# Hybrid encoder step on one core: six low parts per layer through an adding DMA, level products on one engine, other orders at a group's first down units

## What is computed

```python
hn = rmsnorm(x, n1)
proj = hn @ w_in                     # retention q,k,v,g | GLA q,k,v,g,gate | attention q,k,v
a = retention(...)                   # 4 heads, chunks of 64
b = gated_linear_attention(...)      # 4 heads, chunks of 64, decay from a cumulative log gate
c = band_attention(...)              # 8 heads, own chunk and the 8 before
x = x + concat(a, b, c) @ w_out
x = x + square(relu(rmsnorm(x, n2) @ w_up)) @ w_down     # width 4096 inside
```

## Time and profile before

| | us |
|---|---|
| median of 3 runs | 1393.74 (1393.55 to 1395.85) |
| the profiled execution, its own time | 1395.68 |
| its span, first to last instruction | 1393.9 |
| TensorE busy / VectorE / ScalarE / GpSimd | 1344.4 / 947.0 / 643.3 / 155.4 |
| mean granted TensorE clock | 0.991 of full speed |

### The profile page before, as it was taken

The page is one execution under the profiler, slowest core; times in us unless marked ns, Lnnn a source line. Parts: engine busy times, 40 slices in busy tenths (PEclk is TensorE's granted clock), DMA queues, the critical chain, the costliest instruction groups (busy, mean ns, idle before and its releaser), DMA issues. The chain is left out here.

```text
span 1393.9 us, 28762 instructions
## 1 busy us (share of the span) xinstructions
PE 1344.4 (96%) x12206; PEld 1300.3 (93%) x12206; DVE 947.0 (68%) x1480; ACT 643.3 (46%) x1051; POOL 155.4 (11%) x107
## 2 busy tenths in 40 slices
PE   8999999999999999999999999999999999999996
PEld 8899989899999999999998999888999999999995
DVE  6797766778667376575758967667874765746734
ACT  5423555656426236254424236566572362542731
POOL 0200000012120110200202000000201103012012
PEclk9999999999999999999999999999999999999998
DMA  6213333222322323223221223331222232222211
GB/s 227 71 64 103 97 101 116 77 91 76 107 92 78 105 77 106 91 78 105 79 76 48 68 85 120 126 103 63 91 89 95 76 107 91 84 99 92 99 54 64
DMA packets 50640, 127.83 MB, mean 92 GB/s; under 512 B 8401, under 2 KB 17745, under 8 KB 50513
## 3 DMA queue, kind: packets, MB, share of 16 engines
q1 hardware_dynamic: 50224, 125.44, 27.5%
q10 hardware_dynamic: 288, 0.55, 0.1%
HBM read 118.77 MB, written 7.21 MB: 90 GB/s over the span
## 5 line engine op out<-in xcount | busy, mean ns | idle before, releaser
L1698 PE MATMUL PS<-zhi,whi 128*128 128x272 f32 x1280 | 370.0, 289 | 14.0 <-DVE sq L1563 13.6
L1698 PE MATMUL PS<-zhi,wlo 128*128 128x272 f32 x1280 | 370.8, 290 | 0.0
L1698 PE MATMUL PS<-zlo,whi 128*128 128x272 f32 x1280 | 368.8, 288 | 0.0
L999 DVE TENSOR_TENSOR wlo<-raw,whi 128x1024 fp32r<-128x1024 f32 x136 | 169.1, 1243 | 178.3 <-ACT whi L554 177.4
L554 ACT ACTIVATE whi<-raw 128x1024 fp32r<-128x1024 f32 x136 | 143.3, 1055 | 300.1 <-PE PS L1698 295.1
L1698 PE MATMUL PS<-xhi,whi 128*128 128x272 f32 x896 | 271.0, 302 | 6.2 <-DVE wlo L999 3.2
L1698 PE MATMUL PS<-xhi,wlo 128*128 128x272 f32 x896 | 261.1, 291 | 0.0
L1698 PE MATMUL PS<-xlo,whi 128*128 128x272 f32 x896 | 260.5, 291 | 0.0
L1698 PEld LDWEIGHTS PS<-zhi,whi 128*128 128x128 f32 x1280 | 241.3, 188 | 16.1 <-DVE wlo L999 16.0
L1698 PEld LDWEIGHTS PS<-zlo,whi 128*128 128x128 f32 x1280 | 241.6, 189 | 0.0
L1698 PEld LDWEIGHTS PS<-zhi,wlo 128*128 128x128 f32 x1280 | 241.0, 188 | 0.0
(11 more groups left out here) (288 smaller groups left out, 2442.3 us busy)
## 6 DMA issues: line engine op xcount, KB each, us to landing
raw<-in_wu SPq DMA_DIRECT2D x199, 512.0 KB, 3.5
Bh<-in_bias SPq DMA_DIRECT2D x16, 256.0 KB, 4.1
h<-in_x SPq DMA_DIRECT2D x8, 272.0 KB, 6.3
out_k_t<-att_k SPq DMA_DIRECT2D x8, 272.0 KB, 4.3
out_y_t<-y SPq DMA_DIRECT2D x8, 272.0 KB, 2.7
kct<-in_ck SPq DMA_DIRECT2D x8, 256.0 KB, 3.3
cvb<-in_cv SPq DMA_DIRECT2D x8, 256.0 KB, 4.1
out_v_p<-vtk SPq DMA_DIRECT2D x8, 256.0 KB, 2.2
```

The lines of the kernel that those rows point to most:

```text
L999: nc.vector.tensor_tensor(wlo[n % SPL][:, :], raw[n % RAW][:, :], f32(whi[n % SPL][:, :]), ALU.subtract).then_inc(sems["w_lo"], 1)
L1698: return nc.tensor.matmul(out, lhsT, rhs, start=start, stop=stop, skip_group_check=True)
```

## The change

Three things are changed.

1. *Low parts by DMA.* For units 6 to 11 of each layer (`LO_DMA`) VectorE's `rest` is left out. ScalarE, right after `whi`, writes `-whi` into `wlo`; GpSimd then issues a DMA that reads the unit again from HBM and adds it onto `wlo`. `begin` waits for that DMA (semaphores `lo_in0`, `lo_in1`), and SP may load into `raw` again as soon as `whi` is there. Twelve DMAs of 512 KB are added in all.
2. *Levels.* `gk` and `gq` lie in one tile `gkq`, and one VectorE instruction per level makes both halves of `QK` (`level_qk`); GpSimd's `level` goes.
3. *Orders at a group's first down units.* TensorE now does only inputs 0 and 1 of `down+1` before the last two of `down`, and the other six after it. VectorE does `scaled(m - 1)` before `rest(down + m + 1)`. In the first group of a layer `r2` is made before the last pair's `add_c22`, not after the last `zlo`.

```diff
+LO_DMA = range(6, 12)
...
+def by_dma(unit):
+    return unit % UNITS in LO_DMA
...
                         old = unit - RAW
-                        if plain(old) is not None:
-                            sp.wait_ge(sems["w_lo"], plain(old) + 1)
+                        if by_dma(old):
+                            sp.wait_ge(sems["w_hi"], plain(old) + 1)
+                        elif plain(old) is not None:
+                            sp.wait_ge(sems["w_lo"], low(old)[1])
...
-                    def level(l):
...
-                            ins = nc.gpsimd.tensor_tensor(q[:, :, 0, :], f[:, :, 0, :], k[:, :, 0, :], ALU.mult)
-                        ins.then_inc(sems["qk_pool"], 1)
...
+                    for i, n in enumerate(LO_DMA):
+                        pool.wait_ge(sems["w_neg"], nth("w_neg", i + 1))
+                        nc.gpsimd.dma_start(wlo[n % SPL][:, :], wu[layer * UNITS + n, :, :], accum_op=ALU.add) \
+                            .then_inc(sems[f"lo_in{n % SPL}"], 16)
...
                         nc.scalar.activation(whi[n % SPL][:, :], raw[n % RAW][:, :], ACT.Copy).then_inc(sems["w_hi"], 1)
+                        if by_dma(unit):
+                            act.wait_ge(sems["w_hi"], i + 1)
+                            nc.scalar.activation(wlo[n % SPL][:, :], f32(whi[n % SPL][:, :]), ACT.Copy, scale=-1.0) \
+                                .then_inc(sems["w_neg"], 1)
...
-                            f, q, k = (blocks(t, c0, c1, H) for t in (F[l % 2], QK[l % 2], gq))
-                            ins = nc.vector.tensor_tensor(q[:, :, 1, :], f[:, :, 1, :], k[:, :, 1, :], ALU.mult)
-                        ins.then_inc(sems["qk_dve"], 1)
+                            f, qk = (blocks(t, c0, c1, H) for t in (F[l % 2], QK[l % 2]))
+                            kq = gkq[:, c0:c1]
+                            kq = bass.AP(kq.tensor, kq.offset, [kq.ap[0], (2 * H, (c1 - c0) // (2 * H)), (PW + H, 2), (1, H)])
+                            ins = nc.vector.tensor_tensor(qk, f, kq, ALU.mult)
+                        ins.then_inc(sems["qk_ready"], 1)
...
+                            if g == 0 and not more:
+                                dve.wait_ge(sems["ss_all"], nth("ss_all", 1))
+                                nc.vector.tensor_scalar(r2[:, :], rstd[:, :], 1.0 / D, EPS, ALU.mult, ALU.add) \
+                                    .then_inc(sems["r2_steps"], 1)
...
                             add_c22(j)
...
                         for m in range(1, KC):
+                            scaled(m - 1, g)
                             if m < KC - 1:
                                 rest(down + m + 1)
                             elif g == GROUPS - 1:
                                 rest(UNITS)
-                            scaled(m - 1, g)
...
                     def begin(n):
 
+                        name, count = low(layer * UNITS + n)
+                        pe.wait_ge(sems[name], count)
                         unit = plain(layer * UNITS + n)
-                        pe.wait_ge(sems["w_lo"], unit + 1)
...
                         pe.wait_ge(sems["c21"], layer * PAIRS + j)
-                        products(down + 1, (zhi, zlo), all_kc[:6], last=False)
+                        products(down + 1, (zhi, zlo), (0, 1), last=False)
                         products(down, (zhi, zlo), (6, 7), first=False, ready=z_ready)
-                        products(down + 1, (zhi, zlo), (6, 7), first=False)
+                        products(down + 1, (zhi, zlo), all_kc[2:], first=False)
```

More of the change, by code:

```diff
@@ L140, in plain, with low @@
     return None if k < KC else layer * PLAIN + UP + g * KC + k - KC
+def by_dma(unit):
+    return unit % UNITS in LO_DMA
+def low(unit):
+    layer, n = divmod(unit, UNITS)
+    before = min(max(n - LO_DMA.start, 0), len(LO_DMA))
+    if by_dma(unit):
+        return f"lo_in{n % SPL}", PER["lo_in0"] * layer + 16 * (before // SPL + 1)
+    return "w_lo", plain(unit) - len(LO_DMA) * layer - before + 1
 def pair_of(unit):
@@ L255, in hybrid_encoder @@
         Z = 4 * PW
-        gk, gq, gv, gb = (at(n, [P, PW], zone + i * Z) for i, n in enumerate(["gk", "gq", "gv", "gb"]))
+        gkq = at("gkq", [P, 2 * PW], zone)
+        gk, gq = gkq[:, 0:PW], gkq[:, PW:2 * PW]
+        gv, gb = (at(n, [P, PW], zone + i * Z) for i, n in ((2, "gv"), (3, "gb")))
         F = [at(f"F{i}", [P, PW], zone + (4 + i) * Z) for i in range(2)]
@@ L997, in rest @@
                             return
+                        if by_dma(unit):
+                            return
                         dve.wait_ge(sems["w_hi"], plain(unit) + 1)
@@ L1115, in level_x @@
                         if l >= 2:
[L1116 removed]
+                            dve.wait_ge(sems["qk_ready"], nth("qk_ready", l - 1))
                         for g, c0, c1 in level_parts(H):
@@ L1123, in level_x, with level_qk @@
                         ins.then_inc(sems["lev_x"], 1)
-                    def level_q(l):
+                    def level_qk(l):
                         H = LEVELS[l]
@@ L1175, in stage @@
                             if kind == GLA:
-                                level_q(0)
+                                level_qk(0)
                             dve.wait_ge(sems["pe_diag"], nth("pe_diag", kind + 1))
@@ L1200, in stage @@
                             if l + 1 < len(LEVELS):
-                                level_q(l + 1)
+                                level_qk(l + 1)
                             if l + 2 < len(LEVELS):
@@ L1601, in _ @@
                                 sum_s2(j + 1)
+                            if g == 0 and not more:
+                                dve.wait_ge(sems["ss_all"], nth("ss_all", 1))
+                                nc.vector.tensor_scalar(r2[:, :], rstd[:, :], 1.0 / D, EPS, ALU.mult, ALU.add) \
+                                    .then_inc(sems["r2_steps"], 1)
+                                for a in range(2):
+                                    c = slice(a * HT, (a + 1) * HT)
+                                    dve.wait_ge(sems["r2_steps"], nth("r2_steps", a + 1))
+                                    nc.vector.reciprocal(r2[:, c], r2[:, c]).then_inc(sems["r2_steps"], 1)
+                                dve.wait_ge(sems["r2_steps"], nth("r2_steps", 3))
                             add_c22(j)
```

23 lines of the change are left out of this document (6 added, 17 removed).

## The result

The changed kernel took 1373.05 us (median of four executions, 1372.16 to 1375.14) against 1393.64 for the kernel before on the same chip: a ratio of 0.985, 95% interval 0.983 to 0.987. Its profiled execution, the longest of the four, took 1375.14, with a span of 1373.3, 20.6 less than before (1393.9). The prediction was 1375.0 in a range of 1370 to 1388.

What follows compares the result with a forecast made beforehand. TensorE was taken as the bound (busy 1344.4 of 1393.9 us), so only its waits could give time: 1393.9 - 13.6 - 2.9 - 1.6 - 4.0 + 3.0 = 1374.8 of span, from the median 1374.6, say 1375; range 1370 to 1388.

Steps and rivals of the forecast that it cites:

- First down units, -13.6: First down units of the eight groups: TensorE's eight waits of 1.7 us for sq go, -13.6 us.
- Both margins of 0.5 us: In the groups: zlo rows 6 and 7, and c22 before product 4, each ready 0.5 us early, costed at nothing.
- Between the layers, -2.9 and -1.6: Layer boundary: the wait for xlo goes, -2.9 us, and the lower clock right behind it, 694 to 698, -1.6.
- The rival "more": Layer 1's GLA stage: the lower clock there goes too and nothing stalls, 1366 to 1370 us; chance 0.06.
- GLA, VectorE side, -4.0: GLA stage: fewer rest and merged level products shorten waits for QK, Ps and rk, -4.0 us (bounds 0 and -7).
- VectorE's instructions of two inputs there take 1.3 or less: GLA stage: a sign to look for, that VectorE's two-input instructions all take 1.3 us or less.
- The DMAs, +3.0: GLA stage: adding DMAs take 6.5 us, unit 6 stalls 1.4 and unit 10 0.1 a layer, +3.0 (0 to +9.4).
- The other four have over a microsecond more: GLA stage: the DMAs of units other than 6 and 10 have over a microsecond more cover.
- the 8 us: GLA stage, adding DMA: a latency from issue to landing over 8 us would show the prediction wrong.
- The bound of 8.1 for the latency: Adding DMA: upper bound from a 272 KB table load queued at the start, 8.1 us, costing +9.4.
- the clock's half of "partial": GLA stage: idle for late DMAs brings up to two lower-clock episodes a layer, 3.2; whole rival 1380 to 1391, chance 0.20.
- An adding DMA of 9.7 us: Slower rival, GLA stage: at 9.7 us latency the gain is used up, at 12 the time is 1403; chance 0.11.

Runs made afterwards that it cites:

- experiment 5: Kernel before with TensorE's new order of down and down+1 alone, VectorE's orders as before: 1379.31 us, ratio 0.988.
- experiment 6: Kernel before with VectorE's new orders alone (scaled ahead of rest, reciprocals ahead of c22), TensorE's order as before: 1396.71 us, ratio 1.001.
- experiment 9: The changed kernel run once more, unaltered, beside three other variants: 1374.60 us (1372.63 to 1379.27), ratio 0.986.
- Experiment 11: Changed kernel with DMAs for units 7 to 10 alone and SP reloading raw only after the adding DMA has landed: 1368.39 us, ratio 0.981.
- experiment 1: Kernel before with the third part alone (TensorE's order, scaled ahead of rest, reciprocals ahead of c22): 1375.13 us, ratio 0.986.
- experiment 12: Kernel before with the level products on VectorE alone as the only change: 1390.39 us, ratio 0.997.
- experiment 7: Changed kernel with the six DMAs writing plain weights into wlo, the addition left out: 1372.71 us, ratio 0.984.
- experiment 8: Changed kernel with SP loading raw again only when the old unit's adding DMA has landed: 1372.88 us, ratio 0.984.
- 3: Changed kernel with DMAs for units 7 to 10 alone, units 6 and 11 made on VectorE: 1369.85 us, ratio 0.981.

## Why the prediction was right, and where it was off

**First down units, -13.6: right, and too small by 1.6.** A group fell from 92.66 to 90.74, 1.9 in place of the listed 1.7. The view of waits counts from the modelled end of the last matmul, but the next matmul would have begun 0.13 after that one's start, and a matmul lasts 0.29 there. I had used those 0.17 for the spacing and not added them to the gain: 8 x 1.9 = 15.2. Both margins of 0.5 us held. The working also gave VectorE's order a share in it; experiments 5 and 6 show that TensorE's order alone does it.

**Between the layers, -2.9 and -1.6: right.** The boundary fell by 139.08 - 132.43 = 6.65 with the orders alone; less the 1.9 of layer 0's last group, that is 4.75 against 4.5. Here VectorE's order counts: with TensorE's alone 1.9 of the wait stays (experiment 5), and VectorE's alone gives 4.6 of the 4.75 (experiment 6).

**The clock: one of three.** I saw only the stretch in the boundary. The two at 150 and 738 were worth 188.91 - 187.79 = 1.1 and 40.40 - 39.03 = 1.4, and went as well. The rival "more" named one of them. Whether they went because of the change is not shown: the wait for `O` of 1.1 ahead of 150 stands in both kernels, and in experiment 9 the changed kernel has the stretch at 150 again.

**GLA, VectorE side, -4.0: right.** Experiment 11, in which no landing is waited for and four of the six `rest` are gone, has 37.61 and 37.17 where before stood 39.05 and 37.72, and 39.03 and 37.73 in layer 1 without the lower clock (experiment 1): 2.0 a layer, 4.0 in all. 1.25 a layer of it is the levels' part, 0.75 the relief from `rest`. By the waits, the levels alone remove those for QK and Ps L1224 and 0.8 of that for Ps L1183 (experiment 12); that for rk goes only with the `rest`. VectorE's instructions of two inputs there take 1.3 or less, as the prediction asked, but for one `QK` of 1.57 in each layer.

**The DMAs, +3.0: the term that was mis-sized; measured 6.3.** Against experiment 11 the two GLA stages with the parts behind them lose 3.0 in layer 0 and 3.4 in layer 1 (the listed 5.3, some 0.2 for a restart, and in layer 1 an idle 0.49 at 778.64 that the view puts down to issue; its cause is open); in experiment 9's profile, 5.2. Of the listed 5.3, unit 6 took 3.5 where the prediction had 2.8, unit 10 1.1 for 0.2, and unit 11 0.7 for nothing. Its parts were sound at the median: I took 1.3 for the second read, measured 1.7 (experiment 7); 1.3 for the raw load beside it, measured 1.0 (experiment 8); 3.5 + 0.4 for the rest, and 6.6 - 1.7 - 1.0 = 3.9 is left. What failed is that one number stood for all: "The other four have over a microsecond more" and unit 10 at 0.1. Landings took from 5.6 to 8.3, and so unit 11's passed the 8 us that the prediction had named as a sign of being wrong; the median of 6.6 did not. In layer 0 unit 6's, the first, took 60.31 - 53.37 = 6.9; unit 11's took 8.3, issued at 99.88 behind four state stores and a raw load that SP had issued from 97.8 on; unit 10's in layer 1 took 7.3. With the raw loads later (experiment 8) both take 5.6 and don't stall. The bound of 8.1 for the latency was about right, and the range took it in. Why the first landing of a run takes longer in most traces, with or without the addition (6.9 here, 6.8 in experiment 7, 6.6 in 8, but 5.9 in 3), stays open. The Trainium skill's 2.0 us plus bytes at 436 GB/s ("DMA: Bandwidth & Descriptors", "Anatomy of one DMA — SWDGE (gpsimd) path"), an estimate of 3.2 here, was too low for this crowded place: the plain one took 4.9.

**The sum:** -19.1 forecast, -20.6 measured on the profiled executions. That it came out so near is luck, since errors cancel: 1.6 in the groups and 2.5 of clock that I hadn't counted, against 3.3 more for the DMAs.

**Of the rivals,** only the clock's half of "partial" was seen, in single executions and not at the median: the 12 us in experiment 7, and perhaps the 1379.27 of experiment 9, of which only the mean clock is known. An adding DMA of 9.7 us was never seen; the longest took 8.3.

## What to carry to other kernels

Ask of each part of a change what it gives alone: here one reordering of TensorE's list gave most of the gain, and the most elaborate part lost 3 to 5 us until the units with the shortest cover were left out and the competing load was moved; then it gained some 1.6 over none (1.5 by the stages; executions of 1367.98 to 1369.06 against 1369.04 to 1370.27, which only just touch). Price a transfer that is waited for by its slowest landing in the crowded place, not by a median. Moving an instruction of VectorE earlier can start another engine's work beside the next one and give the time back.

## What the runs showed of the hardware that was not expected

A `rest` of 1.22 us takes 2.07 to 2.09 when it starts beside GpSimd's addition. The same program's executions differ by up to 4.7 us (the kernel before), in step with the mean granted clock. Short stretches at the lower level (such as 150 to 156 at a mean of 0.72) come behind waits of 1 to 3 us, at changing ones of them from trace to trace, and cost 1.1 to 1.6 us each (attention 188.91 against 187.79; the boundary, 4.75 less the wait of 2.9 and its 0.17). Once 12 us at a mean of 0.57 followed, behind a wait of 2.02 (experiment 7), while waits of 2.15 and 1.97 for the same unit (the changed kernel, experiment 9) had none behind them. What decides which wait is followed by one was not tried and stays open.
